# Last expert group: gates and ups in two parts around the downs of the group before, its downs by rows and columns

## The chip, the cores and the metric

One core of one Trainium2 chip runs one launch of the program. The metric is the device time of that launch in microseconds. Engines: TensorE (PE, with its weight loads as PEld), VectorE (DVE), ScalarE (ACT), GpSimd (POOL) and SyncE (SP), which issues the loads.

## The reference

A two-layer transformer of width 1024 on 256 tokens. Each layer has three attentions whose outputs are mixed, and then a mixture of 32 experts (4 groups of 8, two experts for each token). The change lies in the experts:

```python
a = jnp.einsum('cd,edf->cef', t, w_gate)      # per expert 1024 x 256
u = jnp.einsum('cd,edf->cef', t, w_up)        # per expert 1024 x 256
hid = (jax.nn.silu(a) * u * combine[..., None]).astype(t.dtype)
return jnp.einsum('cef,efd->cd', hid, w_down) # per expert 256 x 1024
```

All is float32. Each layer reads 96 expert matrices of 1 MB.

## The kernel before

**Tiling.** The 32 experts are worked through in `NGRP` = 8 groups of 4 (these are not the router's groups). Each expert takes up to `CAP` = 32 tokens, so a group fills 128 rows. For a group `g` TensorE does: `gather` (the tokens of the group, turned, into `XT`), `gate_up(g)` (8 steps `k` of the contraction by 4 experts, gate and up side by side, accumulated in bank 4), `turn_hidden(g)` (the hidden rows turned, into bank 4), `turn_weights(g)` (routing weights, bank 7), `down(g)` (two column halves `n`, in each two contraction rows `a` by 4 experts, into banks 5 and 6) and `scatter_group(g)` (back to the tokens, accumulated over all groups in banks 0 to 3, as two column halves by two token tiles). The trace shows a float32 matmul as two instructions: `gate_up` is 64, `down` 32, `scatter_group` 8. ScalarE makes the tanh of the gates and copies the results of `down` from PSUM to `ysb`, half by half. VectorE makes the two products of the hidden rows and copies their turned form. At the end VectorE adds banks 0 to 3 to `x`, each behind its own scatter (`s_fin`).

**Order.** Everything is written out by hand; each engine goes through its program in order and waits on semaphores. For the last two groups TensorE's order is: `gate_up(6)`, `gather(7)`, `turn_hidden(6)`, `turn_weights(6)`, `gate_up(7)`, `turn_hidden(7)`, `down(6)`, `scatter_group(6)`, `turn_weights(7)`, `down(7)`, `scatter_group(7)`.

**Loads.** The matrices are loads `c` = 0 to 95 (`LOADS`) into a ring of 20 slots of 1 MB, all issued by SyncE in `moe_sync` in the order of `c`. `item(c)` names group and matrix: 80 to 87 are gates and ups of group 7, 88 to 91 the downs of group 6, 92 to 95 the downs of group 7. A load waits until its slot was read (`s_gu` counts groups whose gates and ups are done, `s_y` halves of downs). `moe_wait` waits for a load by the semaphore of its slot, `landed[slot]`, against a turn counted at build time. The last four loads are issued by `down_half` as eight column halves of 512 KB, in 2 KB pieces: four first halves on `landed`, four second halves on the shared semaphore `s_side`. A whole gate, up or down has 8 KB pieces. After them come the first four loads of the next layer's attention (behind `s_gu` >= 7), or in layer 1 the final gain of 512 KB.

**Activity.** `keep_warm(pe, n, b)` issues n products of the identity with itself into a bank that nobody reads. `gate_up(7)` has `TAILWARM` = 12 of them between the waits for its sixth and seventh matrix.

Both layers run the same program. A barrier of all engines stands between them.

Of the kernel before, what the change touches and what calls it, by code (L numbers as in the profile page):

```python
# [16 lines left out]
D = 1024  # L17
T = 256
NT = T // P
DEPTH = 2  # L20
KD = D // P
# [16 lines left out]
F = 256  # L38
CAP = 32
NGRP = NE // 4  # L40
# [7 lines left out]
WARM, FILL = 8, 8  # L48
TAILWARM = 12
LOADS = 12 * NGRP  # L50
# [86 lines left out]
def program(nc, A, out, ctx):  # L137
# [8 lines left out]
    ring = sb("ring", [P, SLOTS, SLOT])  # L146
# [117 lines left out]
    cols = tiny(0, 70)  # L264
# [245 lines left out]
    for layer_ in range(DEPTH):  # L510
        for n_ in range(ATT_LOADS):
            count[att_slot(n_)] += 1
            turns_att[layer_, n_] = count[att_slot(n_)]
        for c_ in range(LOADS):
            if not in_extra(c_) and c_ != SIDE:
                count[moe_slot(c_)] += 2 if c_ < 8 else 1
                turns_moe[layer_, c_] = count[moe_slot(c_)]
# [79 lines left out]

    def down_half(sp, layer, c, n, done):

        g, i = item(c)  # L600
        src = A["moe_w_down"][layer, 4 * g + GROUP[i][0]].rearrange("(p j) n -> p j n", j=2)
        slot = ring[:, moe_slot(c), :].rearrange("p (j n) -> p j n", j=2)
        sp.dma_start(slot[:, :, 512 * n:512 * n + 512], src[:, :, 512 * n:512 * n + 512]).then_inc(done, 16)

# [348 lines left out]
    for layer in range(DEPTH):  # L953
# [5 lines left out]
        def moe_wait(eng, c):  # L959

            if c == SIDE:
                eng.wait_ge(s_part, PART + (layer + 1) * 64)
            elif in_extra(c):
                eng.wait_ge(s_side, layer * 112 + 48)
            else:
                eng.wait_ge(landed[moe_slot(c)], turns_moe[layer, c] * 16)
# [1253 lines left out]
        def moe_sync(sp):  # L2220
            for c in range(AHEAD, LOADS - 4):
                g, i = divmod(before_in_slot(c), 12)
                if g == 0 and i < 8:
                    sp.wait_ge(s_g0, i + 1)
                if g and i == 0:
                    sp.wait_ge(s_gu, g)
                if g == 1 and i == 0:
                    load_overflow(sp)
                if i == 8:
                    sp.wait_ge(s_y, 2 * g + 2)  # L2230
                moe_load(sp, layer, c)
            sp.wait_ge(s_gu, NGRP - 2)
            for c in range(LOADS - 4, LOADS):
                down_half(sp, layer, c, 0, landed[moe_slot(c)])
            for c in range(LOADS - 4, LOADS):
                down_half(sp, layer, c, 1, s_side)
            if layer + 1 < DEPTH:
                sp.wait_ge(s_gu, NGRP - 1)
                for n in range(EARLY):
                    attention_load(sp, layer + 1, n)  # L2240
            else:
                sp.dma_start(gfin, A["norm_final"].partition_broadcast(P)).then_inc(f_ld, 16)
# [34 lines left out]
        def moe_tensor(pe):  # L2277
# [151 lines left out]

            def gate_up(g):  # L2430

                pe.wait_ge(s_hde, g)
                for i in range(8):
                    if g == NGRP - 1 and i == 6:
                        keep_warm(pe, TAILWARM, bank[5])
                    moe_wait(pe, place(g, i))
                for k in range(KD):
                    if k % 4 == 0:
                        pe.wait_ge(s_xge, taken(g, k // 4))
                    for e in range(4):  # L2440
# [4 lines left out]
                                         start=(k == 0), stop=(k == KD - 1))  # L2445
                last.then_inc(s_gu, 1)

# [40 lines left out]
            def down(g):  # L2488
# [3 lines left out]
                for n in range(2):  # L2492
                    if n == 1 and 0 < g < NGRP - 1:
                        pe.wait_ge(s_xge, taken(g + 1, 1))
                    if n == 1 and g == NGRP - 1:
                        pe.wait_ge(s_side, layer * 112 + 112)
                    for a in range(2):
                        for e in range(4):
                            last = pe.matmul(down_bank(g, n)[CAP * e:CAP * e + CAP, :],  # L2499
# [3 lines left out]
                    last.then_inc(s_y, 1)  # L2503

            def scatter_group(g):
                pe.wait_ge(s_ste, g + 1)
                for half in range(2):
                    pe.wait_ge(s_ye, 2 * g + half + 1)
                    for t in range(NT):
                        last = scatter(g, t, half)  # L2510
                        if g == NGRP - 1:
                            last.then_inc(s_fin, 1)
                if g < NGRP - 1:
                    last.then_inc(s_scat, 1)

            for g in range(NGRP):
                if g == 3:
                    load_overflow(pe)
                if g == 0:
# [6 lines left out]
                    gather(1, 1)  # L2526
                    continue
                gate_up(g)
                if g <= 2:
# [8 lines left out]
                turn_hidden(g)  # L2538
                if g < NGRP - 1:
                    turn_weights(g)  # L2540
                if g < NGRP - 2:
                    down(g)
                if 1 < g < NGRP - 2:
                    scatter_group(g)

            down(NGRP - 2)
            scatter_group(NGRP - 2)
            turn_weights(NGRP - 1)
            down(NGRP - 1)
            scatter_group(NGRP - 1)  # L2550

        def moe_scalar(act):
# [53 lines left out]
            for g in range(NGRP):  # L2606
# [4 lines left out]
                weights_turned(g)  # L2611
                if g == NGRP - 2:
                    gate_tanh(g + 1)
                if g:
# [390 lines left out]
```

## Time and profile before

| | us |
|---|---|
| median of 3 runs | 1006.33 (1003.88 to 1006.35) |
| the profiled execution | 1001.72 |
| its span, first to last instruction | 999.9 |
| TensorE busy | 925.0 (93% of the span) |
| VectorE, ScalarE, GpSimd busy | 438.8, 253.5, 79.6 |
| mean rate of the loads | 295 GB/s |
| mean granted clock of TensorE | 0.970 of 2.4 GHz |

Busy time of TensorE is modelled at the ends of matmuls, so a busy engine is not one at its peak.
### The profile page before, as it was taken

The page shows a single profiled execution, that of the slowest core. Times are in us where ns is not written, and L with a number is a line of the kernel's source. Part 1 is how long each engine was busy: PE and PEld are TensorE (multiplying, and loading weights), DVE is VectorE, ACT ScalarE, POOL GpSimd, SP SyncE. Part 2 cuts the span into 40 slices and gives each one's busy share as a digit, 9 for nine tenths or more (in the row PEclk, how much of TensorE's full clock was granted, in tenths as well). Part 3 has the DMA queues.
Part 4 walks back from the last instruction along what each step waited for, and adds up shares of the span by engine and source line. Part 5 has one row for each costly group of instructions (what it writes and reads, how often), then busy time and mean ns, then how long its engine had stood idle before and what let it go on. Part 6 is the DMA issues. An engine that isn't in the chain of part 4 may idle for free. (4 is left out here: it accounts for less than half of the span.)

```text
span 999.9 us, 14465 instructions
## 1 busy us (share of the span) xinstructions
PE 925.0 (93%) x5660; PEld 617.9 (62%) x5660; DVE 438.8 (44%) x1094; ACT 253.5 (25%) x716; POOL 79.6 (8%) x122
## 2 busy tenths in 40 slices
PE   9999999999999998677899999999999999986675
PEld 8999778775456543234299987877744655432241
DVE  2644776774773111111144547777478621210012
ACT  2212555552120120000121225565411202100002
POOL 0300010004000000000030000001310000000000
PEclk9999999999999999898999999999999999997888
DMA  9966764539899999999997282447498899999994
GB/s 286 295 211 204 199 174 118 169 122 317 325 365 373 422 422 419 422 420 422 362 334 220 86 269 89 137 116 238 135 368 328 330 417 421 420 421 420 422 414 173
DMA packets 133211, 295.13 MB, mean 295 GB/s; under 512 B 14142, under 2 KB 93076, under 8 KB 111636
## 3 DMA queue, kind: packets, MB, share of 16 engines
q1 hardware_dynamic: 129984, 291.51, 78.6%
q10 hardware_dynamic: 3156, 2.65, 1.6%
q8 instruction: 47, 0.77, 0.3%
q14 instruction: 24, 0.20, 0.1%
HBM read 291.50 MB, written 2.64 MB: 294 GB/s over the span
## 5 line engine op out<-in xcount | busy, mean ns | idle before, releaser
L1381 PE MATMUL bank<-ring,tail 128*128 128x256 f32 x672 | 156.2, 384 | 1.0 <-ACT bank L1655 0.9
L2442 PE MATMUL bank<-ring,tail 128*32 128x512 f32 x896 | 111.3, 654 | 44.9 <-DMA ring<-in_moe_w_up 42.5
L1381 PEld LDWEIGHTS bank<-ring,tail 128*128 128x128 f32 x672 | 124.2, 190 | 25.2 <-issue 9.1
L2788 DVE SCALAR_TENSOR_TENSOR tail<-tail,bank 128x256 f32<-128x256 f32 x16 | 6.7, 421 | 230.0 <-ACT tail L2600 230.0
L2442 PEld LDWEIGHTS bank<-ring,tail 128*32 128x32 f32 x896 | 32.8, 119 | 119.2 <-issue 119.0
L1250 PE MATMUL bank<-tail,ring 128*128 128x128 f32 x672 | 77.1, 276 | 0.0
L1250 PEld LDWEIGHTS bank<-tail,ring 128*128 128x128 f32 x672 | 76.3, 192 | 0.9 <-issue 0.4
L1739 ACT ACTIVATE ring<-ring,small 128x128 f32<-128x128 f32 (+1 forms) x128 | 56.7, 444 | 73.5 <-DVE small L2069 73.5
L1543 PE MATMUL bank<-ring,tail 128*128 128x512 f32 x168 | 73.6, 593 | 0.0
L2499 PE MATMUL bank<-ring,tail 128*32 128x512 f32 x480 | 61.6, 622 | 6.1 <-DVE tail L2801 3.6
L2449 PE MATMUL bank<-tail 128*128 128x512 f32 x128 | 59.2, 605 | 0.0
L2600 ACT ACTIVATE tail<-bank 128x256 f32<-128x256 f32 x16 | 6.1, 384 | 208.7 <-PE bank L2442 187.6
L1543 PEld LDWEIGHTS bank<-ring,tail 128*128 128x128 f32 x168 | 31.4, 190 | 37.7 <-issue 36.7
L2449 PEld LDWEIGHTS bank<-tail 128*128 128x128 f32 x128 | 23.0, 189 | 36.4 <-issue 36.4
L2286 PE MATMUL bank<-ring,tail 128*128 128x512 f32 x96 | 43.9, 597 | 0.9 <-ACT bank L2555 0.5
L2747 DVE TENSOR_TENSOR tail<-bank,small 128x512 f32<-128x512 f32 x30 | 20.6, 688 | 52.3 <-PE bank L2414 52.3
L2414 PEld LDWEIGHTS bank<-tail,x_res 128*128 128x128 f32 x192 | 38.7, 286 | 7.1 <-issue 5.5
L2414 PEld LDWEIGHTS bank<-tail 128*128 128x128 f32 x320 | 36.6, 192 | 7.7 <-issue 7.7
L2414 PE MATMUL bank<-tail,x_res 128*128 128x128 f32 x192 | 40.3, 363 | 1.1 <-DVE tail L2677 1.1
L2499 PEld LDWEIGHTS bank<-ring,tail 128*32 128x32 f32 x480 | 15.5, 114 | 41.1 <-issue 30.1
L2414 PE MATMUL bank<-tail 128*128 128x128 f32 x320 | 38.2, 278 | 0.0
L2273 POOL TENSOR_TENSOR tail<-tail,small 128x128 f32<-128x128 f32 x32 | 12.2, 401 | 320.9 <-PE bank L2479 293.3
(348 smaller groups left out, 1305.9 us busy)
## 6 DMA issues: line engine op xcount, KB each, us to landing
ring<-in_moe_w_up SPq DMA_DIRECT2D x56, 1024.0 KB, 22.0
ring<-in_moe_w_gate SPq DMA_DIRECT2D x56, 1024.0 KB, 20.0
ring<-in_moe_w_down SPq DMA_DIRECT2D x52, 1024.0 KB, 15.2
ring<-in_w_in SPq DMA_DIRECT2D x47, 1024.0 KB, 8.4
ring<-in_w_out SPq DMA_DIRECT2D x8, 1024.0 KB, 7.9
ring<-in_moe_w_down SPq DMA_DIRECT2D x16, 512.0 KB, 16.0
ring<-in_moe_w_gate SPq DMA_DIRECT2D x14, 512.0 KB, 8.9
ring<-in_moe_w_up SPq DMA_DIRECT2D x14, 512.0 KB, 9.2
```

The costliest lines, as they stand in the source:

```text
L1250: last = pe.matmul(dst[:, a * P:(a + 1) * P], weights[:, k, a * P:(a + 1) * P], tokens[:, k, :], start=(fresh and k == 0 and a == 0), stop ...
L1381: last = pe.matmul(dst, tokens[:, k, :], weights[:, k, :], start=False, stop=(k == KD // 2 - 1), skip_group_check=True)
L1543: last = pe.matmul(dst[:, :], tokens[:, c, :], weights[:, 512 * c:512 * c + 512], start=(kind in (1, 5) and c == 0), stop=(c == 1), skip_g ...
L1739: last = act.activation(pr, pr, ACT.Exp, scale=scale, bias=mx[:, c:c + 1], accum_out=sm[:, c:c + 1])
L2273: last = pool.tensor_tensor(Sw[:, t, :].rearrange("p (e c) -> p e c", c=CAP), picked(gr)[:, t], bc(weight, [P, 4, CAP]), ALU.mult)
L2286: last = pe.matmul(dst, tokens[:, k, :], weights[:, k, :], start=(start and k == 0), stop=(k == 3), skip_group_check=True)
L2414: last = pe.matmul(b[:, (k % 4) * P:(k % 4 + 1) * P], rows_k, Sel[:, g % 2, t, :], start=(t == 0 and k % 4 == 0), stop=(t == NT - 1), skip ...
L2442: last = pe.matmul(bank[4][CAP * e:CAP * e + CAP, :].rearrange("p (a f) -> p a f", a=2), XT[:, k, CAP * e:CAP * e + CAP], ring[:, lo:hi + ...
L2449: return pe.matmul(bank[2 * t + half][:, :], ST[:, t * P:(t + 1) * P], ysb[:, 512 * half:512 * half + 512], start=(g == 0), stop=(g == NGR ...
L2499: last = pe.matmul(down_bank(g, n)[CAP * e:CAP * e + CAP, :], hidden_rows(g)[:, a, CAP * e:CAP * e + CAP], moe_home(place(g, 8 + e))[:, a ...
L2747: dve.tensor_tensor(XT[:, 4 * half:4 * half + 4, :], bank[7 - half][:, :].rearrange("p (a c) -> p a c", a=4), bc(gain, [P, 4, P]), ALU.mul ...
L2788: s(dve.scalar_tensor_tensor(out=hid[:, 0, :], in0=hid[:, 0, :], scalar=1.0, in1=bank[4][:, 0:F], op0=ALU.add, op1=ALU.mult))
```

## The change

Gates and ups of group 7 are loaded as two halves by contraction (`k` 0 to 3 and 4 to 7, 512 KB each in 4 KB pieces). The first halves keep the place of the whole matrices in the queue, the second ones come after the downs of group 6, on the shared semaphore `s_part`. The downs of group 7 are loaded as first contraction rows whole (`a` = 0, 512 KB, 4 KB pieces), then the second rows' first 512 columns (256 KB, 2 KB pieces), both on `landed`, then the second rows' last 512 columns on `s_side`.

TensorE's order becomes: `gate_up(6)`, `gather(7)`, `turn_hidden(6)`, `turn_weights(6)`, first half of `gate_up(7)`, 6 keeping products, `down(6)`, `scatter_group(6)`, `turn_weights(7)`, 8 keeping products, second half of `gate_up(7)`, `turn_hidden(7)`, `down(7)`, second half of the scatter of 7. The first half of that scatter stands inside `down(7)`, ahead of the last part (`n` = 1, `a` = 1) and of its wait for `s_side`. ScalarE copies the turned weights of group 7 before the tanh of its gates.

```diff
-TAILWARM = 12
+TAILWARM, GROUPWARM = 8, 6
@@
-                count[moe_slot(c_)] += 2 if c_ < 8 else 1
+                count[moe_slot(c_)] += 2 if c_ < 8 or c_ >= LOADS - 4 else 1
@@
-    def down_half(sp, layer, c, n, done):
+    def gate_half(sp, layer, c, part, done):
+
+        g, i = item(c)
+        e, m = GROUP[i]
+        src = A["moe_w_gate" if m == 0 else "moe_w_up"][layer, 4 * g + e].rearrange("(p k) f -> p (k f)", k=KD)
+        r = slice(4 * F * part, 4 * F * part + 4 * F)
+        sp.dma_start(ring[:, moe_slot(c), r], src[:, r]).then_inc(done, 16)
+
+    def down_part(sp, layer, c, row, cols, done):
...
-        sp.dma_start(slot[:, :, 512 * n:512 * n + 512], src[:, :, 512 * n:512 * n + 512]).then_inc(done, 16)
+        sp.dma_start(slot[:, row, cols], src[:, row, cols]).then_inc(done, 16)
@@
-                eng.wait_ge(s_part, PART + (layer + 1) * 64)
+                eng.wait_ge(s_part, PART + layer * 192 + 64)
@@
-                moe_load(sp, layer, c)
+                if LOADS - 16 <= c < LOADS - 8:
+                    gate_half(sp, layer, c, 0, landed[moe_slot(c)])
+                else:
+                    moe_load(sp, layer, c)
+            for c in range(LOADS - 16, LOADS - 8):
+                gate_half(sp, layer, c, 1, s_part)
             sp.wait_ge(s_gu, NGRP - 2)
             for c in range(LOADS - 4, LOADS):
-                down_half(sp, layer, c, 0, landed[moe_slot(c)])
+                down_part(sp, layer, c, 0, slice(0, D), landed[moe_slot(c)])
             for c in range(LOADS - 4, LOADS):
-                down_half(sp, layer, c, 1, s_side)
+                down_part(sp, layer, c, 1, slice(0, 512), landed[moe_slot(c)])
+            for c in range(LOADS - 4, LOADS):
+                down_part(sp, layer, c, 1, slice(512, D), s_side)
@@
-            def gate_up(g):
-
-                pe.wait_ge(s_hde, g)
-                for i in range(8):
-                    if g == NGRP - 1 and i == 6:
-                        keep_warm(pe, TAILWARM, bank[5])
-                    moe_wait(pe, place(g, i))
-                for k in range(KD):
+            def gate_up(g, ks=range(KD)):
+
+                if 0 in ks:
+                    pe.wait_ge(s_hde, g)
+                    for i in range(8):
+                        moe_wait(pe, place(g, i))
+                else:
+                    keep_warm(pe, TAILWARM, bank[5])
+                    pe.wait_ge(s_part, PART + layer * 192 + 192)
+                for k in ks:
@@
-                last.then_inc(s_gu, 1)
+                if KD - 1 in ks:
+                    last.then_inc(s_gu, 1)
@@
-                    if n == 1 and g == NGRP - 1:
-                        pe.wait_ge(s_side, layer * 112 + 112)
                     for a in range(2):
+                        if n == 1 and a == 1 and g == NGRP - 1:
+                            pe.wait_ge(s_ste, g + 1)
+                            scatter_half(g, 0)
+                            pe.wait_ge(s_side, layer * 112 + 112)
@@
+                if g == NGRP - 1:
+                    gate_up(g, range(0, 4))
+                    continue
@@
+            keep_warm(pe, GROUPWARM, bank[5])
             down(NGRP - 2)
             scatter_group(NGRP - 2)
             turn_weights(NGRP - 1)
+            gate_up(NGRP - 1, range(4, KD))
+            turn_hidden(NGRP - 1)
             down(NGRP - 1)
-            scatter_group(NGRP - 1)
+            scatter_half(NGRP - 1, 1)
@@
                 weights_turned(g)
-                if g == NGRP - 2:
-                    gate_tanh(g + 1)
+                if g == NGRP - 1:
+                    gate_tanh(g)
```

`scatter_half(g, half)` is the inner part of the old `scatter_group(g)`: the wait for ScalarE's copy of that half and the scatter to both token tiles.

## Rows read from the trace of the kernel before

**Rows 1.** The page: TensorE's busy tenths and the loads' GB/s in 40 slices.
```profile
PE   9999999999999998677899999999999999986675
...
GB/s 286 295 211 204 199 174 118 169 122 317 325 365 373 422 422 419 422 420 422 362 334 220 86 269 89 137 116 238 135 368 328 330 417 421 420 421 420 422 414 173
```

**Rows 2.** Timeline, layer 1: start, duration, engine, line, operation, [idle before <- releaser].
```profile
942.95 8.49 PE L2442 MATMUL bank<-ring,tail 128*32 128x512 f32 x64 [8.31 <-DMA ring<-in_moe_w_up]
...
955.48 0.42 DVE L2801 COPY tail<-bank 128x256 f32<-128x256 f32 x1 [0.43 <-PE bank L2485]
...
963.54 7.07 PE L2442 MATMUL bank<-ring,tail 128*32 128x512 f32 x64 [0.38 <-issue]
...
972.56 0.42 DVE L2801 COPY tail<-bank 128x256 f32<-128x256 f32 x1 [0.60 <-PE bank L2485]
973.53 5.12 PE L2499 MATMUL bank<-ring,tail 128*32 128x512 f32 x32 [1.00 <-DMA ring<-in_moe_w_down]
...
978.59 3.70 PE L2449 MATMUL bank<-tail 128*128 128x512 f32 x8
...
982.12 0.38 PE L2479 MATMUL bank<-cst,tail 128*128 128x128 f32 x2
982.44 1.92 PE L2499 MATMUL bank<-ring,tail 128*32 128x512 f32 x16
...
984.83 1.92 PE L2499 MATMUL bank<-ring,tail 128*32 128x512 f32 x16 [0.47 <-DMA ring<-in_moe_w_down]
986.68 3.70 PE L2449 MATMUL bank<-tail 128*128 128x512 f32 x8
986.82 0.60 ACT L2618 ACTIVATE tail<-bank 128x512 f32<-128x512 f32 x1 [1.73 <-PE bank L2499]
```

**Rows 3.** Timeline, the same columns, layer 0.
```profile
467.20 2.92 PE L608 MATMUL bank<-cst 128*128 128x128 f32 x24 [0.87 <-DMA ring<-in_moe_w_up]
...
482.13 5.07 PE L2499 MATMUL bank<-ring,tail 128*32 128x512 f32 x32 [1.01 <-DMA ring<-in_moe_w_down]
...
490.98 3.83 PE L2499 MATMUL bank<-ring,tail 128*32 128x512 f32 x32
...
494.74 3.70 PE L2449 MATMUL bank<-tail 128*128 128x512 f32 x8
```

**Rows 4.** Downs' issues, and for each in order KB and us to landing.
```profile
945.45 2.14 SPq L569 DMA_DIRECT2D ring<-in_moe_w_down  x1
ring<-in_moe_w_down SPq DMA_DIRECT2D x1, 1024.0 KB, 27.9
...
972.85 1.25 SPq L603 DMA_DIRECT2D ring<-in_moe_w_down  x1
ring<-in_moe_w_down SPq DMA_DIRECT2D x1, 512.0 KB, 11.9
```

**Rows 5.** Windows: stretch, busy us of each engine, granted clock, DMA share, GB/s.
```profile
960.00:970.00 10.00, 9.62 (x77) 5.35 (x78) 0.00 (x0) 0.00 (x0) 0.00 (x0) 0.85 1.01 422
...
976.60:980.00 3.40, 3.40 (x24) 1.10 (x17) 0.00 (x0) 1.19 (x2) 0.00 (x0) 1.00 1.05 387
```

**Rows 6.** Timeline, other groups: downs without a wait, gates and ups after one.
```profile
436.38 3.64 PE L2499 MATMUL bank<-ring,tail 128*32 128x512 f32 x32 [0.30 <-DVE tail L2801]
...
913.10 9.75 PE L2442 MATMUL bank<-ring,tail 128*32 128x512 f32 x64 [9.19 <-DMA ring<-in_moe_w_up]
```

**Rows 7.** Windows before and at the downs of group 6 (clock: third number from the end).
```profile
969.60:973.00 3.40, 1.52 (x14) 0.42 (x6) 1.27 (x3) 0.38 (x1) 0.00 (x0) 1.00 1.00 390
973.20:976.40 3.20, 2.87 (x16) 0.91 (x20) 0.00 (x0) 0.00 (x0) 0.00 (x0) 0.50 1.05 387
```

**Rows 8.** Layer 0: SyncE's first attention load, its landing and its reader.
```profile
482.69 1.22 SPq L530 DMA_DIRECT2D ring<-in_w_in  x1
ring<-in_w_in SPq DMA_DIRECT2D x1, 1024.0 KB, 14.0
...
501.72 7.07 PE L1280 MATMUL bank<-ring,tail 128*128 128x256 f32 x32
```

More of the change, by code:

```diff
@@ L2503, in down, with scatter_half @@
                     last.then_inc(s_y, 1)
+            def scatter_half(g, half):
+                pe.wait_ge(s_ye, 2 * g + half + 1)
+                for t in range(NT):
+                    last = scatter(g, t, half)
+                    if g == NGRP - 1:
+                        last.then_inc(s_fin, 1)
+                return last
             def scatter_group(g):
                 pe.wait_ge(s_ste, g + 1)
[L2507 to L2514, printed above, removed]
+                scatter_half(g, 0)
+                scatter_half(g, 1).then_inc(s_scat, 1)
             for g in range(NGRP):
@@ L2538, in moe_tensor @@
                 turn_hidden(g)
-                if g < NGRP - 1:
-                    turn_weights(g)
+                turn_weights(g)
                 if g < NGRP - 2:
@@ L2611, in moe_scalar @@
                 weights_turned(g)
-                if g == NGRP - 2:
-                    gate_tanh(g + 1)
+                if g == NGRP - 1:
+                    gate_tanh(g)
                 if g:
```

## The prediction

> **What bounds the kernel now.** I read the page first [rows 1]: TensorE counts as busy for nine tenths in most slices, but in the second layer's experts, slices 33 to 38 of 40, the DMA engines are full (417 to 422 GB/s), and TensorE falls to 6 to 8 tenths from the 36th. The weights set the pace there. Then the timeline of the last two groups of layer 1, where the change lies [rows 2]. Group 6's gates and ups (64 matmuls) wait 8.31 us for a transfer and end at 951.44; group 7's run from 963.54 to 970.61, behind twelve products that only keep the engine active. Its hidden rows are turned and copied by 972.98. Group 6's downs then wait 1.00 us for a down-projection and start at 973.53. From there TensorE hardly stops: downs of 6 (5.12 us), scatter of 6 (3.70), weights turned (0.38), first column half of group 7's downs (1.92), 0.47 us of wait, second half (1.92), scatter of 7 (3.70), end 990.38. VectorE's last addition is queued right behind. Layer 0 repeats it 491.4 us earlier, downs of 6 from 482.13, and ends at 498.44 [rows 3]; there the whole downs of 7 take 3.83 us without a gap.
>
> So two things end together. TensorE has 16.4 us of work behind 973.53, and the last transfer also comes late. Issue time plus time to landing [rows 4]: group 6's last down lands at 945.45 + 27.9 = 973.35, the eighth and last half of group 7's downs at 972.85 + 11.9 = 984.75. From 984.83 to the end are 5.55 us.
>
> **What the change moves.** It takes TensorE work out from behind 973.53. Group 7's gates and ups come in two halves by k. The order of transfers is now: eight first halves, group 6's four downs, eight second halves, then group 7's downs as four whole first rows, four first column halves of the second rows, four last ones. The bytes are the same. The slices of the page that cover 925 to 975 carry 422 and 414 GB/s, no hole [rows 1], so each transfer lands where its place in the byte order puts it.
>
> *First halves.* All eight whole matrices landed by 963.5. Their second halves are 4.19 MB, 9.9 us at 422 GB/s, so the first halves are there at about 953.6. TensorE's own work behind group 6's gates is done by then plus 2 us, and the copy of the hidden rows out of bank 4 ends at 955.90 [rows 2]: 32 matmuls, half of 7.07, run 955.95 to 959.5. They fill about half of the empty time ahead of 963.54. The six products that keep it active take 1.5 us (24 instructions in 2.92 us at full clock in layer 0 [rows 3]), to 961.0.
>
> *Downs of 6.* Eight halves and four downs are as many bytes as the eight whole matrices were, so they start at about 963.9, wait near 2.9 us: 3.64 us at full clock [rows 6], then scatter 3.70 and weights 0.38, end 971.6. ScalarE takes the results between, as now. Eight more keeping products (1.95 us) end at 973.6.
>
> *Second halves.* They land where group 6's downs did, 973.35, plus 0.6 us (next paragraph): 974.0. 32 matmuls to 977.6, then tanh, two products, turn and copy, which took 972.98 - 970.61 = 2.37 us: hidden rows ready at 980.0. If the 2.9 us wait drops the clock, the downs of 6 take 5.12 instead of 3.64 and this is 981.3, since only 0.4 us of it is cover ahead of 974.0.
>
> *Transfers.* A load with 2 KB per row piece moves 387 GB/s (column halves, 976.6 to 980), one with 8 KB 422 (whole matrices, 960 to 970) [rows 5]. For 4 KB pieces, which the halves and the first rows have, no row stands alone; bounds 387 and 422. Taking a fixed cost per piece and one per byte through the two ends gives 410, which I take. 8.39 MB of halves: 20.5 instead of 19.9 us, +0.6. First rows, 2.10 MB, leave 2 KB pieces: 5.1 instead of 5.4 us, -0.3. The last landing is then 984.75 + 0.3 = 985.05 (bounds 984.3 and 986.6). 
>
> *The last stage.* The downs of 7 still wait for both landings of their slots, first rows and first columns, before their first instruction. What follows those in the queue is 1.05 MB of last columns, 2.7 us at 387 GB/s. They can start at 985.05 - 2.7 = 982.35, plus the 0.1 us from landing to start seen at 984.75/984.83. That is later than the hidden rows (980.0 to 981.3), so the transfer decides. Before, this stage needed half of those bytes, about 979.3 by the queue, and TensorE was the one that came late (982.44); now three quarters must be in. Behind it in order on TensorE: first column half 1.82 (1.92 less the tail that overlaps the next), first-row part of the second half 0.91, scatter of the first half 1.76, the last part 0.91 + 0.2, then a stop that was not there: ScalarE must copy that half (0.07 + 0.60 + 0.07 us; before, the scatter of the first half covered it, now it has gone ahead), and the scatter of the second half 1.76 + 0.14. Sum 8.24. The wait for the last columns, 985.05, is passed at 982.45 + 4.49 = 986.9 and costs nothing. End 990.7, against 990.38: +0.3. Layer 0 repeats the sequence to 0.5 us, so I take +0.3 there too.
>
> *The clock.* In the new order TensorE is empty before this stage from 977.6 to 982.45, but for turning the hidden rows, two products. The present wait behind gates and ups, 970.61 to 973.53 with only the turning in it, already took the granted clock from 2.4 to 1.2 GHz: 1.00 in 969.6 to 973.0, 0.50 in 973.2 to 976.4 [rows 7]. Price: 5.12 - 3.64 = 1.5 us in layer 1, 5.07 - 3.64 = 1.4 in layer 0. After waits of 8.31 and 9.19 us, 64 matmuls took 8.49 and 9.75 instead of 7.07: 1.4 and 2.7 [rows 2, 3, 6]. A wait of 4.8 us lies between; I take 2.0, bounds 1.0 and 2.7. It was paid at the downs of 6 before, where the wait for the last half (0.47 us) absorbed a part; now it falls wholly behind the deciding transfer. Nothing keeps the engine active in this gap: both groups of keeping products are ahead of gates and ups. The Trainium skill, "TensorE: Matmul & The Clock Gate", section "HAM oscillation — how this bites in real kernels", describes matmuls that wait for a transfer and then start at half rate each time, the loss being half of the slow time. The trace agrees: some 3 us at 0.50 cost 1.5 us.
>
> *SyncE and the rest.* SyncE issues 12 more transfers, at 1.2 us or so each where little holds it back; what holds it is the full queue, in which a transfer takes 12 to 28 us from issue to landing [rows 4, 8]. The wait for group 6's gates stays where it was. In layer 0 the next layer's first loads wait for the end of gates and ups of 7, now about 486.2 or 487.5 instead of 479.3; SyncE reached them at 482.69 [rows 8]. The last downs land at 492.8, so the queue still has work then; the first of these loads landed at 482.69 + 14.0 = 496.7 and is read at 501.7. A hole of 2 us would be hidden by those 5. SyncE's later loads stand behind the barrier between the layers, which moves with TensorE's end by the same 2.3 us.
>
> **Sum.** Per layer +0.3 for the later start and the uncovered copy, +2.0 for the clock: +2.3. Twice: +4.6 us. The profiled execution is 1001.72 (span 999.9 and 1.8 around it), so 1006.3; it lies 4.6 below the median of the runs, 1006.33, and on that the forecast is 1010.9.
>
> **Rivals.** *No change:* the clock is back before this stage or drops little, or the first columns land a microsecond earlier. For it: the phase of the clock differs, 1.4 against 2.7 after equal waits. Against it: both layers paid it after a shorter gap. Per layer 0.3 - 0.5 to 0.3 + 1.0, in all -0.4 to +2.6, middle 1007.4. *Faster:* the last columns, not the first ones, decide. From 984.75 only 0.1 + 0.91 + 0.2 + 0.74 + 1.9 = 3.85 us are left instead of 5.55, end 988.6 to 988.9: -1.5 to -1.8 per layer, 1003.0. This holds only if the downs start at full clock by 985.05 - 4.49 = 980.6, with the first columns in 1.8 us ahead of their place in the queue. For it speaks that the whole four downs landed 11.4 us after group 6's, where 4.19 MB at 387 GB/s are 10.8: landings stray by half a microsecond; 1.8 is more than that. *Much slower:* the hidden rows become the limit. The second part of gates and ups runs at the low clock after the two waits, 32 matmuls in up to 7.07 us: ready at 983.5, end 991.8 plus what is left of the low clock, +3.5 per layer, 1013.3. It decides once the parts before lose more than 2.4 us. *The split does nothing:* if TensorE couldn't begin the first halves before 963, all would shift by the 3.5 us that were to fill the gap; that is the same time as the last case, and I count it there.
>
> **Chances.** Forecast (slower by 3 to 6.5 us) 0.52; no change 0.27; faster 0.12; much slower 0.09. A measurement of this kernel can tell about 0.3%, 3.0 us, from no change. Part of the forecast's case lies under 3 us and part of the no-change case over it, about as much: slower 0.60, same 0.28, faster 0.12. The range leaves out most of the faster case and the far end of the slowest: 1004.5 to 1014.0; the forecast's own is 1009.3 to 1012.8.
>
> **What would show it.** Right: 32 gate and up matmuls right behind 955.9; downs of 6 at about 963.9; downs of 7 started by a down-projection's landing at 982 to 982.6; clock 0.50 in their first microseconds; about 0.9 us of TensorE idle before the last scatter. Wrong: downs of 7 started by the hidden rows' copy, a start before 981, clock 1.00 there, or a queue with a hole near 490.

## The result and the profile after

The changed kernel takes 1007.93 us (median of 14 runs, 1006.28 to 1015.74), the kernel before 1003.67 (14 runs, 1001.54 to 1006.89; the three runs that stood ahead of the prediction are among them and lay high). The ratio is 1.0045, 95% interval 1.0031 to 1.0059: 4.5 us slower, 3.1 to 5.9. Forecast were +4.6 us.

The profiled execution of the changed kernel took 1015.74 us (span 1014.0), one of its two longest, so spans can't be compared. A mark common to all traces can: the start of group 6's gates and ups, which a landing sets. It is 452.40 and 942.95 before [rows 2] and 455.78 and 954.94 after. Times "from the mark" are counted from there.

Timeline of TensorE after, layer 1:

```profile
954.94 8.62 PE L2459 MATMUL bank<-ring,tail 128*32 128x512 f32 x64 [8.19 <-DMA ring<-in_moe_w_up]
...
968.08 3.64 PE L2459 MATMUL bank<-ring,tail 128*32 128x512 f32 x32 [0.30 <-DVE tail L2828]
971.65 1.60 PE L616 MATMUL bank<-cst 128*128 128x128 f32 x12
974.98 3.64 PE L2519 MATMUL bank<-ring,tail 128*32 128x512 f32 x32 [1.72 <-DMA ring<-in_moe_w_down]
978.55 3.70 PE L2467 MATMUL bank<-tail 128*128 128x512 f32 x8
...
982.30 1.95 PE L616 MATMUL bank<-cst 128*128 128x128 f32 x16
985.12 3.64 PE L2459 MATMUL bank<-ring,tail 128*32 128x512 f32 x32 [0.87 <-DMA ring<-in_moe_w_up]
990.18 0.51 PE L2503 MATMUL bank<-cst,tail 128*128 128x128 f32 x2 [1.42 <-DVE tail L2820]
993.16 5.35 PE L2519 MATMUL bank<-ring,tail 128*32 128x512 f32 x24 [2.47 <-DMA ring<-in_moe_w_down]
998.44 2.28 PE L2467 MATMUL bank<-tail 128*128 128x512 f32 x4
...
1000.65 1.07 PE L2519 MATMUL bank<-ring,tail 128*32 128x512 f32 x8
...
1002.43 1.98 PE L2467 MATMUL bank<-tail 128*128 128x512 f32 x4 [0.72 <-ACT tail L2645]
```

SyncE's last part of the downs there, from the timeline, and from the DMA issues its KB and us to landing; ahead of it the last part of the first columns:

```profile
979.40 0.43 SPq L611 DMA_DIRECT2D ring<-in_moe_w_down  x1
ring<-in_moe_w_down SPq DMA_DIRECT2D x1, 256.0 KB, 13.6
...
985.15 1.08 SPq L611 DMA_DIRECT2D ring<-in_moe_w_down  x1
ring<-in_moe_w_down SPq DMA_DIRECT2D x1, 256.0 KB, 10.4
```

The reader sees the predicted order with its waits. The first halves of gates and ups fill the empty time (968.08); the downs of 6 start at 20.0 from the mark instead of 30.6 and run at full clock; the second halves end at 988.76. Then TensorE has two turning products in 4.4 us, until a down-projection lands: the last of the first columns, at 979.40 + 13.6 = 993.00. The downs of 7, 24 instructions up to the scatter inside them, take 5.35 us. Before the last scatter stand 0.72 us of waiting for ScalarE, which the kernel before doesn't have [rows 2]. The last part lands at 985.15 + 10.4 = 995.55, long before it is read at 1000.65.

Layer 0 after:

```profile
455.78 9.03 PE L2459 MATMUL bank<-ring,tail 128*32 128x512 f32 x64 [9.45 <-DMA ring<-in_moe_w_up]
...
493.86 4.47 PE L2519 MATMUL bank<-ring,tail 128*32 128x512 f32 x24 [2.37 <-DMA ring<-in_moe_w_down]
...
502.01 1.98 PE L2467 MATMUL bank<-tail 128*128 128x512 f32 x4 [0.72 <-ACT tail L2645]
```

From the mark the last scatter ends at 48.21 in layer 0 and 49.47 in layer 1; before, at 46.04 and 47.43: +2.2 and +2.0 us. Together that is 4.2 of the 4.5 us of measured loss, by one profile of each kernel; the next section has a second profile of the changed one.

Windows after (third number from the end: granted clock), which answer to [rows 7] and [rows 5]:

```profile
988.90:993.10 4.20, 0.51 (x2) 0.31 (x2) 1.27 (x3) 0.32 (x1) 0.00 (x0) 0.90 1.05 390
993.20:996.50 3.30, 3.30 (x16) 0.83 (x20) 0.00 (x0) 0.00 (x0) 0.00 (x0) 0.50 0.38 149
...
493.90:497.00 3.10, 3.10 (x16) 0.91 (x20) 0.00 (x0) 0.00 (x0) 0.00 (x0) 0.50 1.07 364
...
975.00:985.00 10.00, 9.25 (x58) 4.62 (x58) 0.00 (x0) 1.58 (x3) 0.00 (x0) 1.00 1.03 409
```

In layer 1 the clock falls to 1.2 GHz at the end of the gap (0.90 over the gap) and stays there through the start of the downs; layer 0 (third row) starts its downs at 1.2 GHz too. The last row is the rate of 4 KB pieces, 409 GB/s, between the 387 and 422 of 2 and 8 KB pieces.

### The profile page after: what moved, and what is told of

Read it like the earlier page. It is cut to its first block and busy times, and to the rows that moved or that the text cites. A ratio compares the mean times of both kernels' runs of the same rounds, so it can differ in the third digit from the quotient of the medians.

```text
span 1014.0 us, 14509 instructions
## 1 busy us (share of the span) xinstructions
PE 929.3 (92%) x5668; PEld 617.6 (61%) x5668; DVE 439.6 (43%) x1094; ACT 253.1 (25%) x716; POOL 78.6 (8%) x122
## 3 DMA queue, kind: packets, MB, share of 16 engines
q10 hardware_dynamic: 3156, 2.65, 1.6%
## 5 line engine op out<-in xcount | busy, mean ns | idle before, releaser
L1551 PEld LDWEIGHTS bank<-ring,tail 128*128 128x128 f32 x168 | 31.4, 190 | 37.7 <-issue 36.7
L2429 PEld LDWEIGHTS bank<-tail,x_res 128*128 128x128 f32 x192 | 38.7, 286 | 7.1 <-issue 5.5
L2645 ACT ACTIVATE tail<-bank 128x512 f32<-128x512 f32 x32 | 19.1, 597 | 77.9 <-PE bank L2519 77.9
```

Source lines behind the costliest of these rows:

```text
L1551: last = pe.matmul(dst[:, :], tokens[:, c, :], weights[:, 512 * c:512 * c + 512], start=(kind in (1, 5) and c == 0), stop=(c == 1), skip_g ...
L2429: last = pe.matmul(b[:, (k % 4) * P:(k % 4 + 1) * P], rows_k, Sel[:, g % 2, t, :], start=(t == 0 and k % 4 == 0), stop=(t == NT - 1), skip ...
L2645: act.activation(ysb[:, 512 * n:512 * n + 512], down_bank(g, n)[:, :], ACT.Copy).then_inc(s_ye, 1)
```

## The experiments

Each was timed beside the kernel before (10 to 12 runs of the version, 23 or 35 of the kernel before) and profiled once. The versions were run in four sets, each with its own runs of the kernel before: changed kernel again, active gap, downs' parts alone and gates' split alone; covered copy, rows first, its empty gap and other products out; waits active 3 and 6 with parts alone, copy covered; waits active 1 and 4 with the covered copy again. Edits are shown against the changed kernel where nothing else is said. The table gives the ratio to the kernel before, and from the mark the start of the downs of 7 and the end of the last scatter, layer 0 / layer 1.

| version | ratio (95% interval) | start | end |
|---|---|---|---|
| kernel before (profile above) | 1 | 38.58 / 39.49 | 46.04 / 47.43 |
| changed kernel (profile above) | 1.0045 (1.0031 to 1.0059) | 38.08 / 38.22 | 48.21 / 49.47 |
| changed kernel again | 1.0026 (1.0012 to 1.0039) | 38.12 / 38.82 | 48.91 / 49.52 |
| gap kept active | 1.0004 (0.9989 to 1.0019) | 39.10 / 38.29 | 47.53 / 46.72 |
| downs' parts alone | 0.9997 (0.9984 to 1.0011) | 38.58 / 39.09 | 47.02 / 47.52 |
| gates' split alone | 1.0023 (1.0008 to 1.0038) | 37.33 / 37.00 | 49.94 / 47.74 |
| active gap, copy covered | 0.9980 (0.9965 to 0.9995) | 39.69 / 38.64 | 47.01 / 45.92 |
| the same again | 0.9978 (0.9963 to 0.9993) | 38.45 / 38.56 | 45.77 / 45.83 |
| rows first | 0.9999 (0.9982 to 1.0016) | 36.30 / 37.05 | 47.72 / 46.02 |
| rows first, gap empty | 0.9991 (0.9979 to 1.0002) | 37.95 / 36.55 | 47.91 / 45.94 |
| rows first, waits active 3 and 6 | 0.9989 (0.9973 to 1.0004) | 36.36 / 37.06 | 46.42 / 47.00 |
| rows first, waits active 1 and 4 | 0.9982 (0.9966 to 0.9999) | 36.56 / 36.36 | 46.16 / 45.41 |
| active gap, other products out | 1.0011 (0.9995 to 1.0026) | 39.16 / 38.58 | 47.60 / 47.01 |
| parts alone, copy covered | 0.9999 (0.9977 to 1.0021) | 37.89 / 40.39 | 45.22 / 47.66 |

Starts and ends are those of one execution each, and the profiled execution of the kernel before (1001.72 us) lies 2 to 4 us under the medians of its runs. Measured against it, the ends put the versions 0.8 us later on average than the times do, in one case 2.4. They show where time goes in a stage; how much a version gains or loses is told by the ratio.

**The changed kernel again.** No edit.

> The changed kernel itself, as the mark for the others of this set. My theory (the last stage starts at the landing of the second rows' first columns, and starts at the low clock): from the start of group 6's gates and ups, which a landing sets and which is the mark common to all traces, the downs of 7 start 38.2 us later and the last scatter ends 49 to 50 us later (47.4 in the kernel before), in both layers. +3.5 to +5 us against the kernel before. The rival (the loss lies elsewhere, in the extra transfers or in the next layer's attention, whose first loads are issued later): the last scatter ends within 1 us of the kernel before by that mark, and the rest appears after the barrier.

Starts and ends are near what I expected (38.12 and 38.82, 48.91 and 49.52). The 24 instructions take 5.18 and 5.09 us. The time is less than expected: 2.6 us slower (1.2 to 3.9) instead of 3.5 to 5, against 4.5 (3.1 to 5.9) in the comparison above; the intervals overlap. The rival, that the loss lies in the next layer's attention, falls: from the last scatter of layer 0 to the first products of layer 1 that read a loaded weight (`L1280` before, `L1288` here) it is 3.3 us in both kernels (498.44 to 501.72 before, 502.23 to 505.52 here).

**Gap kept active.**

```diff
+            keep_warm(pe, 5, bank[5])
             turn_hidden(NGRP - 1)
+            keep_warm(pe, 9, bank[5])
             down(NGRP - 1)
```

> The changed kernel with 5 more keeping products ahead of turning group 7's hidden rows and 9 behind it, so that TensorE is active in the gap ahead of the downs of 7. My theory: granted clock 1.00 in the downs of 7, which take 3.8 us or so less the waits instead of 4.5 to 5.4; the last scatter ends 1 to 2 us earlier in each layer than in the changed kernel; in all 2 to 4 us faster than it, +0 to +2 against the kernel before. The rival (the clock is not what costs; place in the queue and the uncovered copy are): at most 0.5 us faster than the changed kernel.

Its timeline in layer 1, with the keeping products as L616:

```profile
980.88 0.51 PE L2503 MATMUL bank<-cst,tail 128*128 128x128 f32 x2
981.22 2.17 PE L616 MATMUL bank<-cst 128*128 128x128 f32 x18
983.75 2.78 PE L2519 MATMUL bank<-ring,tail 128*32 128x512 f32 x24 [0.35 <-DMA ring<-in_moe_w_down]
986.53 1.95 PE L2467 MATMUL bank<-tail 128*128 128x512 f32 x4
```

and the window of those downs (columns as in [rows 7]):

```profile
983.70:986.50 2.80, 2.75 (x24) 0.81 (x24) 0.00 (x0) 0.60 (x1) 0.00 (x0) 1.00 0.59 230
```

Clock 1.00, the same 24 instructions in 2.78 us instead of 4.47 to 5.35, and from start to end 8.43 us in both layers instead of 10.13, 11.25, 10.79 and 10.70. The start still waits for a down-projection. 2.9 us faster than the changed kernel beside it (medians 1004.86 against 1007.72) and level with the kernel before. The rival, that queue and copy are what costs, allowed 0.5 us and falls. What is left for them is 0.4 us per layer by the ends, the mean of +1.5 and -0.7: in layer 0 of this profile the last columns land at 41.73 from the mark, 1.1 us later than in the changed kernel, so a single layer of one profile can't tell it. By the times it is 0.4 us in all, -1.1 to +1.9.

**Downs' parts alone.** Whole gates and ups, TensorE's order and the twelve keeping products of before; rows, columns and the scatter inside the downs stay as changed.

```diff
-                if LOADS - 16 <= c < LOADS - 8:
-                    gate_half(sp, layer, c, 0, landed[moe_slot(c)])
-                else:
-                    moe_load(sp, layer, c)
-            for c in range(LOADS - 16, LOADS - 8):
-                gate_half(sp, layer, c, 1, s_part)
+                moe_load(sp, layer, c)
...
-                if g == NGRP - 1:
-                    gate_up(g, range(0, 4))
-                    continue
...
-            gate_up(NGRP - 1, range(4, KD))
-            turn_hidden(NGRP - 1)
```

> Only the second part of the change: the downs of 7 in rows and columns with the scatter's first half inside them; gates and ups of 7 whole, TensorE's order as in the kernel before. My theory: TensorE arrives at the downs of 7 straight from the scatter of 6, at about 39.5 us after group 6's gates start, when the first columns are in; full clock; the uncovered copy of 0.7 us takes the place of the 0.47 us wait: -0.5 to +0.6 us per layer, -1 to +1.2 in all. The rival (the smaller transfers and the split order of the downs cost by themselves): as slow as the changed kernel, +3 or more.

Level with the kernel before (by the ends +1.0 and +0.1). TensorE comes from the scatter of 6 (layer 0, no wait) or waits 1.27 us (layer 1), and the 24 instructions take 2.78 us in both. The smaller transfers of the downs and their split order cost nothing that can be measured.

**Gates' split alone.**

```diff
-                down_part(sp, layer, c, 0, slice(0, D), landed[moe_slot(c)])
+                down_part(sp, layer, c, slice(0, 2), slice(0, 512), landed[moe_slot(c)])
...
-                down_part(sp, layer, c, 1, slice(512, D), s_side)
+                down_part(sp, layer, c, slice(0, 2), slice(512, D), s_side)
```

with the wait for `s_side` ahead of the second column half and both halves of the scatter behind the downs.

> Only the first part of the change: gates and ups of 7 in halves by contraction around the downs of 6, with both groups of keeping products; the downs of 7 as two column halves, scatter behind them, as in the kernel before. My theory: the downs of 7 are ready at their hidden rows or at the first column halves, about 37 us after group 6's gates start, after a gap of 2.5 us; a low clock there is hidden by the wait for the last halves; from there 5.6 us to the end: the last transfer decides, 0 to +0.8 us per layer, 0 to +1.6 in all. The rival (the split of the gates loses the time): +3 us or more.

+2.3 us, between the two expectations: I expected the last landing to decide and the clock to be hidden. Layer 1 did that (+0.3 by the ends): the first column half ran at the low clock, 3.59 us, ahead of the wait. Layer 0 ended 3.9 us later than before; timeline:

```profile
490.18 1.92 PE L2515 MATMUL bank<-ring,tail 128*32 128x512 f32 x16 [0.52 <-DVE tail L2826]
495.59 3.25 PE L2515 MATMUL bank<-ring,tail 128*32 128x512 f32 x16 [3.49 <-DMA ring<-in_moe_w_down]
498.77 4.02 PE L2465 MATMUL bank<-tail 128*128 128x512 f32 x8
```

and the window of the second column half:

```profile
495.60:499.00 3.40, 3.40 (x17) 0.80 (x18) 0.00 (x0) 0.12 (x1) 0.00 (x0) 0.57 0.97 238
```

TensorE did the first column half at full clock and then waited 3.49 us for the last halves, now the only wait long enough; the clock fell there, and 3.25 + 4.02 us stand where 1.92 + 3.70 did. Coming early moved the wait to the place where nothing hides the slow start. This is my theory's mechanism at another place than I expected it. By the ends of this one profile the two layers lose 4.2 us together, by the times 2.3.

**Active gap, copy covered.** The edit of the active gap, and

```diff
                         if n == 1 and a == 1 and g == NGRP - 1:
-                            pe.wait_ge(s_ste, g + 1)
-                            scatter_half(g, 0)
                             pe.wait_ge(s_side, layer * 112 + 112)
...
             down(NGRP - 1)
+            pe.wait_ge(s_ste, NGRP)
+            scatter_half(NGRP - 1, 0)
             scatter_half(NGRP - 1, 1)
```

> The changed kernel with the active gap of the run before (5 and 9 keeping products), and the last part of the downs of 7 ahead of both halves of the scatter, so that the scatter's first half covers ScalarE's copy of the second half again. My theory: from the start of the downs of 7 to the end of the last scatter 7.5 to 7.7 us instead of the 8.43 of the run with the active gap alone, since 0.74 us of copy is covered and the last columns (2.6 us behind the first ones) land just before they are read: 0.7 us per layer, 1.5 us in all faster than that run, -1 to -2.5 against the kernel before. The rival (the last columns land too late for this order, and TensorE waits for them what it saves in copy): same as the run with the active gap alone.

> The version with the active gap and the covered copy once more, unchanged, since the best of several versions may be best by luck. My theory: 0.1% to 0.3% faster than the kernel before again, last stage 7.3 us from the start of the downs of 7 to the end. The rival (its lead of 0.2% was luck): ratio 0.9990 or above.

Timeline of the first, layer 1, TensorE and ScalarE:

```profile
983.25 3.64 PE L2517 MATMUL bank<-ring,tail 128*32 128x512 f32 x32 [0.35 <-DMA ring<-in_moe_w_down]
985.30 0.60 ACT L2647 ACTIVATE tail<-bank 128x512 f32<-128x512 f32 x1 [5.87 <-PE bank L2517]
986.83 3.70 PE L2467 MATMUL bank<-tail 128*128 128x512 f32 x8
986.95 0.60 ACT L2647 ACTIVATE tail<-bank 128x512 f32<-128x512 f32 x1 [1.06 <-PE bank L2517]
```

The second copy runs under the first half of the scatter, which goes on without a stop: 7.3 us from start to end in all four layers instead of 8.43; 7.5 to 7.7 were expected. Twice faster than the kernel before, by 2.0 and 2.2 us in 1005, with intervals that leave 1 out both times. This is the version that beats both kernels; one other does (below, rows first with 1 and 4 products), on one set of runs.

**Rows first.** The four parts of the downs of 7 in the order of their landing, the second rows' first columns on a semaphore of their own, scatter behind.

```diff
+                order = ((0, 0), (1, 0), (0, 1), (1, 1)) if g == NGRP - 1 else ((0, 0), (0, 1), (1, 0), (1, 1))
+                for n, a in order:
...
+                        if g == NGRP - 1 and a == 1:
+                            if n == 0:
+                                pe.wait_ge(s_uk, layer * 80 + 80)
+                            else:
+                                pe.wait_ge(s_side, layer * 112 + 112)
```

5 keeping products ahead of the turning and 3 behind it; without these eight in the version with the empty gap.

> The changed kernel with the downs of 7 in the order in which their parts land: both column halves of the first rows (waiting only for the first rows), then the second rows' first columns, which have a semaphore of their own, then their last columns, then both halves of the scatter. 5 keeping products ahead of turning the hidden rows and 3 behind. My theory: by the mark of group 6's gates start, the downs of 7 start at 36.5 to 37 (hidden rows ready at 36.2, first rows landed at about 35.2), at full clock, and after 40.7 (last columns) only 0.9 + 0.2 + 3.7 us are left, end 45.4 to 46.6: 1.5 to 3.5 us faster than the kernel before. The rival (TensorE was never what decided; only the last landing does, and the order can't help): no faster than the kernel before.

> The same without the eight keeping products in the gap, so the wait of some 2.7 us between gates and ups and downs of 7 is empty but for turning the hidden rows. My theory of the clock: it drops in the gap or just behind it in most layers, the first-row parts take up to 3.6 us instead of 1.9, but most of that is hidden ahead of the last columns at 40.7: 0 to 1.5 us slower than with the products. The rival (the clock falls only in gaps of 4 us and more): same as with them, and 1.00 in the downs of 7.

The first was a miss: starts at 36.3 and 37.05 as expected, but as slow as the kernel before. Layer 1 ended at 46.02, in the expected range; layer 0 did not. Its timeline there:

```profile
492.19 1.92 PE L2521 MATMUL bank<-ring,tail 128*32 128x512 f32 x16
494.76 1.07 PE L2521 MATMUL bank<-ring,tail 128*32 128x512 f32 x8 [0.64 <-DMA ring<-in_moe_w_down]
497.48 1.94 PE L2521 MATMUL bank<-ring,tail 128*32 128x512 f32 x8 [1.65 <-DMA ring<-in_moe_w_down]
499.34 4.27 PE L2467 MATMUL bank<-tail 128*128 128x512 f32 x8
```

and the window of the last part:

```profile
497.50:500.00 2.50, 2.50 (x9) 0.68 (x10) 0.00 (x0) 0.52 (x1) 0.00 (x0) 0.50 1.13 304
```

Waits of 0.64 and 1.65 us with 1.07 of work between them were enough to lose the clock, behind the last landing, where each slow product counts: 1.94 + 4.27 instead of 1.06 + 3.70, 1.5 us. The version with the empty gap lost it earlier (24 instructions of the first three parts in 4.48 us in both layers instead of 2.78), where it is mostly hidden, and had it back for the last part (1.06). So by the times it is not slower, as I had it, but as fast or faster. Its ends are no earlier (47.91 and 45.94): in layer 0 the clock had also fallen at the downs of 6 (5.34 us behind a wait of 2.08), and the last columns landed late, at 43.2 from the mark.

**Rows first, waits active.** Keeping products also ahead of the two waits inside the downs, 3 and 6 in the first version, 1 and 4 in the second (the edit is shown against rows first).

```diff
                             if n == 0:
+                                keep_warm(pe, 3, bank[4])
                                 pe.wait_ge(s_uk, layer * 80 + 80)
                             else:
+                                keep_warm(pe, 6, bank[4])
                                 pe.wait_ge(s_side, layer * 112 + 112)
```

> The rows-first order again (first rows of both halves, second rows' first columns, last columns, scatter), now with 3 keeping products ahead of the wait for the first columns and 6 ahead of the wait for the last ones, in which layer 0 of the earlier run lost its clock. My theory: clock 1.00 through the last stage in both layers, last part at the last landing (40.6 to 41.7 from the mark), end 4.8 us behind it, 45.4 to 46.5 against 46.04 and 47.43 before: 1 to 3 us faster than the kernel before. The rival (the clock was not what that run lost): no faster than the kernel before.

> The rows-first order with 1 and 4 keeping products in its two waits instead of 3 and 6, of which the six ended 0.9 us behind the last landing in layer 1. My theory: the last part starts within 0.1 us of the last landing (41.0 to 41.7 from the mark) at full clock in both layers, end at 45.9 to 46.5; 1 to 2 us faster than the kernel before and level with the version that covers the copy. The rival (with so few products the clock falls again): low clock in the last part in one layer or more, no faster than the kernel before.

With 3 and 6 the last part took 1.06 us in both layers, and the time is 1.1 us below the kernel before, at the lower edge of the 1 to 3 us that I expected, with an interval of -2.7 to +0.4. In layer 1 the products were too many: the last columns had landed at 41.33 from the mark and the part started at 42.31, behind them. With 1 and 4 it starts at 41.46 in layer 0 and 40.71 in layer 1, at full clock (1.06 and 1.07 us), the end in layer 1 is the earliest of all, and the ratio is 0.9982: level with the covered copy, by another way, though the interval leaves 1 out only just and the version was run once. By the profiles the clock was what layer 0 of the first version of this order had lost; the times of the three versions don't separate them.

**Active gap, other products out.** The edit of the active gap, and

```diff
-TAILWARM, GROUPWARM = 8, 6
+TAILWARM, GROUPWARM = 0, 0
```

> The run with the active gap (5 and 9 products ahead of the downs of 7) without the 6 and 8 keeping products that the change has ahead of the downs of 6 and of the second part of gates and ups. My theory: the downs of 6 may start at the low clock (1.5 us longer), but the hidden rows have 2 us to spare ahead of the first columns' landing, so the end stays within 0.5 us of the run with the active gap. The rival (hidden rows decide): 1.5 to 3 us slower.

The second part of gates and ups waited 2.65 us in both layers; in layer 0 the clock fell (5.12 us instead of 3.64), in layer 1 not:

```profile
482.51 5.12 PE L2459 MATMUL bank<-ring,tail 128*32 128x512 f32 x32 [2.65 <-DMA ring<-in_moe_w_up]
...
975.01 3.64 PE L2459 MATMUL bank<-ring,tail 128*32 128x512 f32 x32 [2.66 <-DMA ring<-in_moe_w_up]
```

In layer 0 the downs of 7 then started right behind the keeping products (39.16), no longer at a landing. The ends are 0.1 and 0.3 us later than with the products: they protect something with little to lose.

**Parts alone, copy covered.** The edit of the downs' parts alone together with the second edit of the covered copy (wait without the scatter inside the downs, both scatters behind them).

> Only the loads of the downs of 7 in rows and columns, the wait for the last columns ahead of the last part, both halves of the scatter behind it; gates and ups whole and TensorE's order as in the kernel before. If the split of gates and ups is worth something once its gap is active and the copy covered, this is slower than that version (which was 0.2% faster than the kernel before). My theory: it is worth little: TensorE reaches the downs of 7 at 38.6 to 39.5 from the mark, the first columns land at 38 to 39; end 46.0 to 46.9: -0.5 to -1.5 us against the kernel before. The rival (splitting the gates is what gains): as the kernel before.

1006.08 us at the median, 999.76 to 1008.2, ratio 0.9999 with the widest interval of all: it can't be told from the kernel before, and not clearly from the covered copy either. Its runs fall into two groups: four at 999.8 to 1000.7, below every run of the kernel before and of the covered copy, and eight at 1004.3 to 1008.2. The profile (1007.28) is of the second group; none of the four was profiled, so what sets them apart stays open. In the profile the clock fell in layer 0 at the gates and ups of 7 (8.77 us instead of 7.07), and in layer 1 at the downs of 6 (5.34 us), where TensorE was then late (start at 40.39, no wait). Whether the split of the gates is worth something stays open: the four shortest times speak against it, the median for it. Its ends, 46.44 on average, are level with those of the first covered version (46.47) and 0.6 us behind the second (45.80).

## Why the prediction was right, and where its sizes were off

**The fill of the empty time.** Right. The 32 first instructions run 13.1 to 16.8 from the mark (forecast 13.0 to 16.6), the downs of 6 from 20.0 (21.0), the hidden rows are copied at 36.2 (forecast 37.0).

**The clock ahead of the downs of 6.** I gave a fall there 1.3 us on the hidden rows (981.3; by the prediction's own terms, 1.5 less 0.4 of cover, it is 1.1). In the two profiles of the changed kernel it didn't fall: 3.64 us in all four layers.

**Transfers.** 4 KB pieces move 409 GB/s where I took 410. The landings were forecast 0.7 to 1.5 us too late: first columns at 39.4 from the mark, measured 37.9 to 38.7; last columns at 42.1, measured 40.67 and 40.61 (in the second profile 40.67 and 41.21). I had built on layer 1's last landing before (41.8) and set it for both layers; the trace had layer 0's at 40.4, 1.4 us earlier. The distance from first to last columns was right, 2.7 us forecast and 2.5 to 2.8 measured. So the last stage started at 38.1 to 38.8, not 39.5.

**The last stage.** 8.24 us forecast at full clock, 8.43 measured with the active gap. The uncovered copy is 0.72 us in every version that has it. The step held, and it was worth removing: 1.1 us per layer from start to end.

**The clock.** The step that carries the forecast, and right: 0.50 behind a gap of 4.3 to 5.0 us with two turning products in it, in all four layers profiled. Forecast 2.0 us per layer, measured against 8.43: 1.7, 2.8, 2.4 and 2.3, mean 2.3. That it was this and not the place in the queue is shown by the active gap: the same order and the same wait for a landing, clock 1.00, and 2.9 us less time.

**The sum.** +0.3 + 2.0 per layer was forecast. Measured at the ends: +2.2 and +2.0, or +2.9 and +2.1 in the second profile. Two mis-sized terms offset each other: the start came earlier than forecast, the clock cost more. So that +4.6 and +4.5 us meet to a tenth is luck in part; the second set of runs gave 2.6, under the 3 us with which the forecast's case begins, though its interval reaches to 3.9. The forecast in absolute time, 1010.9, is 3.0 above the measured median because the three runs of the kernel before that it was set on lay 2.7 above the median of its 14.

**Rivals.** *Faster* needed a start at full clock by 37.7 from the mark (980.6): it came at 38.1 at the earliest, at the low clock. *Much slower* needed the hidden rows later than the first columns: they were 2 us ahead. SyncE's later loads cost nothing in these profiles: in layer 0 the first attention load was issued at 489.64 and landed 9.8 us later, at 499.4, ahead of its reader at 510.4 (in the second profile 498.5 and 505.5). The hole in the queue near 490, a sign of being wrong, didn't come: 395 and 379 GB/s in 488 to 492 and 492 to 496.

## What to carry to other kernels

Work that is moved forward leaves its gap somewhere, and the gap is worth what stands behind it: ask of every wait of TensorE whether the next landing still has slack behind it, and fill those that have none with products that nobody reads, no more of them than end before the landing. When a load is cut so that TensorE can start early, the part that decides is the last landing that the first instruction waits for and all work queued behind it, so order the work as the parts land and keep a copy out of PSUM under other matmuls.

## What I had not expected of the hardware

The clock fell after less than I would have thought: in layer 0 of rows first after waits of 0.64 and 1.65 us with 1.07 us of work between (its layer 1, with one wait of 1.49 us, kept it), in one layer of two after a wait of 2.65 us (active gap, other products out), and in one layer of two after waits of 2.08 and 1.82 us (rows first, gap empty: 5.34 and 3.64 us at the downs of 6). Nearly the same wait in the same kernel has both outcomes, and each of these falls costs 1.5 to 1.7 us of TensorE, which shows in the time where nothing behind it hides it.

In the profiled execution of the changed kernel TensorE stood still for 2.81 us between two transposes right behind the barrier of layer 1, in a run of like products that wait for nothing that the profile shows:

```profile
505.63 1.64 PE L1157 MATMUL bank<-cst,x_res 128*128 128x128 f32 x13 [1.64 <-PEq L2845]
510.08 0.49 PE L1157 MATMUL bank<-cst,x_res 128*128 128x128 f32 x3 [2.81 <-issue]
```

No other profile of these kernels has it. It lies outside the change and is one part of the 8 us by which that execution is over its median. What caused it stays open.
